# Two more feed-forward groups as seven block products, with low-part buffers of their own, another home for one sum, and reordered closings

## The chip, the cores and the metric

One core of a Trainium2 chip runs the whole program. The metric is device time in microseconds for one execution, lower is better. The kernel before was timed three times: 2315.58, 2322.17 and 2316.37 us, median 2316.37 us.

## The reference

The computation is a two-layer decoder trunk on 512 tokens of width 1024, all in float32. Every layer applies half a SwiGLU feed-forward, a token mixer, cross-attention into 256 memory tokens, and another half SwiGLU. The change is in the first half of the feed-forwards:

```python
def swiglu(x, w_gate, w_up, w_down):
    return (jax.nn.silu(x @ w_gate) * (x @ w_up)) @ w_down

def half_ffn(h, l, j):
    y = swiglu(rms_norm(h, ffn_norm_pre[l, j]), ffn_w_gate[l, j], ffn_w_up[l, j], ffn_w_down[l, j])
    return h + 0.5 * rms_norm(y, ffn_norm_post[l, j])
```

There are four feed-forwards, (layer, half) = (0,0), (0,1), (1,0), (1,1), with 2816 hidden columns each. Cross-attention uses `rms_norm(mem, mem_g) @ w_kv` in both layers, so the memory tokens are needed once in each layer.

## The kernel before

**Precision.** Each float32 operand is split into a high and a low part, and each product is three matmuls: low x high, high x low, high x high (lines 2447 to 2449 and 2565 to 2570). A weight tile of 128 x 1024 numbers (a "piece") is loaded into one of four raw slots, ScalarE copies its high part into `whi`, and the low part goes into `wlo`; both have four slots. Usually VectorE makes the low part as raw minus high (line 1503). ScalarE and VectorE split a piece three pieces ahead of TensorE (LOOKAHEAD).

**Groups.** The hidden columns are taken 256 at a time, so a feed-forward has eleven groups, in three stages: groups 0 to 2, groups 3 to 5, groups 6 to 10. After each of the first two stages a "quads" pass multiplies its three groups into the output (also by seven block products). Pass 0 is the opening pass, where ScalarE copies five of its products out of PSUM (line 1283) and VectorE adds the others (line 1599). After the third stage comes the plain down projection.

A plain group is 4 pieces of 24 matmuls of 512 columns, 96 in all. A group as seven block products ("woven") is 7 units of 24 matmuls of 256 columns, 168 in all. Before, groups 6 to 10 of the feed-forwards (0,1), (1,0) and (1,1) are woven, 15 groups in all.

**A woven group.** TensorE's units are, in order, B11, T1, T2, B21, T3, B22, T4. Four raw loads feed them, B11, B12, B22, B21, each of two DMAs of 256 KB on SyncE's queue. T1 to T4 are sums that VectorE makes in place in the raw slots (lines 1522, 1526, 1530, 1535: T1 = B12 - B11, T2 = B22 - T1, T3 = T2 - B11, T4 = B21 - T2). Before, T1, T2 and T4 all live in B12's slot. The next load into a slot waits for the last thing made from it.

The low parts of T1 to T4 are made by VectorE. Those of B11, B21 and B22 are made by DMA: ScalarE writes the negated and rounded copy of raw into the `wlo` slot (line 896) and the high part into `whi` (line 899); then GpSimd issues a DMA that adds raw onto the negated copy (line 792, "an add"), which leaves the low part. Each add moves 512 KB.

Between units, ScalarE copies three products out of PSUM ("keep", line 1195, after B11, T1 and T2). TensorE waits for the first before T2, for the third before T3, and for VectorE's sum c22 (line 2023) before T4. At a group's end ScalarE applies silu to the last product (line 1220) and VectorE multiplies (line 2036, "the product"). ScalarE's first keep of the next group waits for that product. In stage three ScalarE then splits the product at once (`plain_hi`, line 1163); in stage two VectorE would first make four block sums (lines 1944 to 1950), and ScalarE and VectorE split two parts (lines 1168, 1173, 1955, 1961).

**Order around the change.** Every engine runs its own list in program order, and SyncE's DMAs are issued in program order too. While the loads of the second group of stage two are issued, SyncE also issues the nine "corner" loads of the coming quads pass (w11, w12, w21, three DMAs of 256 KB each, line 624): w11's behind the group's first load, w12's behind the second, w21's behind the third.

**Closings.** Before the feed-forwards (0,1), (1,0) and (1,1) a closing finishes the sublayer row tile by row tile: VectorE updates h (line 1719), multiplies by the gain (1727) and forms the input variance (1760), GpSimd raises it to -1/2 (line 797; line 787 for the result's own variance), ScalarE scales the rows (988), TensorE transposes them (2529).

Of the kernel before, what the change touches and what calls it, by code (L numbers as in the profile page):

```python
# [35 lines left out]
D = 1024  # L36
SEQ = 512
MEM = 256
# [21 lines left out]
N_FF = FF // 256  # L60
MID_SLOTS = QUADS
S1, S2, S3, S4, A12, A22, A11 = range(7)
WOVEN = (6, 7, 8, 9, 10)
WOVEN_UNITS = ("B11", "T1", "T2", "B21", "T3", "B22", "T4")
WOVEN_SUMS = ("T1", "T2", "T3", "T4")
WOVEN_CORNERS = ("B11", "B12", "B22", "B21")
# [63 lines left out]
O_BANK = [6, 7, 4, 5]  # L130


def build(nc, A, out, h_kept):
    f32, f32r, bf16, i8 = mybir.dt.float32, mybir.dt.float32r, mybir.dt.bfloat16, mybir.dt.int8
    ALU, ACT, AX = mybir.AluOpType, mybir.ActivationFunctionType, mybir.AxisListType
    MUL, ADD, SUB = ALU.mult, ALU.add, ALU.subtract
# [31 lines left out]
    wlo = place("wlo", [P, SPLIT_SLOTS, PK, GC], f32r)  # L168
    memT_at = top[0]
    memT = place("memT", [P, KT, MEM])  # L170
    ring_at = top[0]
    ring = place("ring", [P, 4, SEQ])
    y_scratch = place("y_scratch", [P, 2, GC], f32, ring_at)
# [116 lines left out]
    raw_full = [sem(f"raw_full{i}") for i in range(RAW_SLOTS)]  # L290

    hi_made, lo_made, pieces_used = map(sem, ("hi_made", "lo_made", "pieces_used"))
    raw_added = [sem(f"raw_added{i}") for i in range(SPLIT_SLOTS)]
    corners_summed, s_made, s_hi_ready, s_lo_ready = map(sem, ("corners_summed", "s_made", "s_hi_ready", "s_lo_ready"))
    h_stored, h_back = sem("h_stored"), sem("h_back")
    product_kept, c11_ready, c11_silu, c22_ready = map(sem, ("product_kept", "c11_ready", "c11_silu", "c22_ready"))
# [51 lines left out]
    S_HELD_IN = [R22, R11, R21, R12]  # L348
    S_MADE = [0, 2, 1, 3]
    S_HIGH_AT = [6, 7, 8, 9]  # L350
    s_low = lambda s: s_lo_early[:, s] if s < 3 else s_lo_last[:]


# [75 lines left out]
        return slice(g * GC, (g + 1) * GC)  # L429

    raw_of, raw_split, passes = [], [], []
    sum_at, corner_unit, corner_raw, lo_by_dma, woven_base, woven_group = {}, {}, {}, set(), [], {}
    for n_stage, (kind, l, arg, ng, n) in enumerate(STAGES):
        if kind != "quads":
            for g in range(ng):
                if not woven(kind, l, arg, g):
                    for _ in range(group_pieces(kind, g, n, arg, l)):
                        raw_of.append(len(raw_split))
                        raw_split.append((len(raw_of) - 1,))
                    continue  # L440
                base, raw0 = len(raw_of), len(raw_split)
                unit = {name: base + i for i, name in enumerate(WOVEN_UNITS)}
                corner = {name: raw0 + i for i, name in enumerate(WOVEN_CORNERS)}
                held_in = {"B11": "B11", "B21": "B21", "B22": "B22", "T1": "B12", "T2": "B12", "T3": "B11", "T4": "B12"}
                raw_of += [corner[held_in[name]] for name in WOVEN_UNITS]
                raw_split += [(unit["T3"],), (unit["T4"],), (unit["B22"],), (unit["B21"], unit["T4"])]
                for name in WOVEN_SUMS:
                    sum_at[unit[name]] = len(sum_at) + 1, name, unit, corner
                lo_by_dma |= {unit[name] for name in WOVEN_BY_DMA}
                woven_group[n_stage, g] = len(woven_base)  # L450
                woven_base.append(base)
            continue
        place_of = lambda name, q: len(raw_of) + piece_of(quad_units().index((name, q)))
        passes.append((len(raw_of), len(raw_split), FF_GROUPS[arg[1]][0]))
        raw_split += [(place_of("B22", min(q + 1, QUADS - 1)),) for q in range(0, QUADS, 2)]
        raw_of += [None] * n

    def woven_first_of(w):
# [3 lines left out]
    def await_lo(eng, n):  # L462

        if n in lo_by_dma:
            eng.wait_ge(raw_added[n % SPLIT_SLOTS], 16 * sum(m in lo_by_dma for m in range(n % SPLIT_SLOTS, n + 1, SPLIT_SLOTS)))
        else:
            eng.wait_ge(lo_made, RAW_SLOTS + sum(m not in lo_by_dma for m in range(n + 1)))

# [112 lines left out]
    def _(sp):  # L581
# [18 lines left out]
        def load(n, halves):  # L600


            slot = n % RAW_SLOTS
            if n >= RAW_SLOTS:
                for m in raw_split[n - RAW_SLOTS]:
                    await_lo(sp, m)
            for dst, src in halves(slot):
                sp.dma_start(dst, src).then_inc(raw_full[slot], 16)

# [61 lines left out]
        def keep_h():  # L671

            kept[0] += 1
            sp.wait_ge(rows_scaled, TT * kept[0])
            for half in range(2):
                sp.dma_start(h_kept[half * HALF:(half + 1) * HALF].rearrange("(t p) d -> p t d", p=P),
                             h[:, 2 * half:2 * half + 2, :]).then_inc(h_stored, 16)

        def restore_h():

            sp.wait_ge(h_stored, 32 * kept[0])
            for half in range(2):
                sp.dma_start(h[:, 2 * half:2 * half + 2, :],
                             h_kept[half * HALF:(half + 1) * HALF].rearrange("(t p) d -> p t d", p=P)).then_inc(h_back, 16)

        kept = [0]
        piece = ended = loads = 0
# [82 lines left out]
    def _(pool):  # L770
# [17 lines left out]

        def add_raw(n):

            pool.wait_ge(hi_made, n + 1)
            g.dma_start(wlo[:, n % SPLIT_SLOTS], raw[:, raw_of[n] % RAW_SLOTS], accum_op=ADD).then_inc(raw_added[n % SPLIT_SLOTS], 16)

        def input_power(t):

# [38 lines left out]
        for n_stage, (kind, l, arg, ng, np_) in enumerate(STAGES):  # L834
            base_piece = E.piece
            for n in range(base_piece, base_piece + stage_pieces(kind, l, arg, ng, np_)):
                if n in lo_by_dma:
                    add_raw(n)
            E.piece += stage_pieces(kind, l, arg, ng, np_)
            if from_h(kind, arg) and not scaled_rows(kind, l, arg):  # L840
                power(TT, 0, rstd_in, var_in)
            if base_piece == 0:
                power(MT, 8)
            if kind == "even_in":
                make_tables()


                power(16)
                for _ in range(4):
                    power(TT)  # L850
                E.made[ring_summed.name] += KT
                E.seen[ring_squared.name] += KT
            elif kind == "odd_in":
                E.await_(conv_ready)
                for c in range(1, CONV_T):
                    E.await_(conv_ready)
                    if c > 1:
                        E.own()
                    E.run(g.tensor_tensor(ring[:, 0, :], conv[:, 0, :] if c == 1 else ring[:, 0, :], conv[:, c, :],
                                          ADD), conv_added)  # L860
                power(TT)
                E.made[ring_summed.name] += CONV_T
                E.seen[ring_squared.name] += CONV_T
            elif ends_sublayer(kind, arg) and opens_scaled(n_stage):
                power(1, 0)
                input_power(0)
                power(1, 1)
                input_power(1)
                power(1, 2)
                power(1, 3)  # L870
                input_power(2)
                input_power(3)
            elif ends_sublayer(kind, arg):
                for t in range(TT):
                    power(1, t)
# [3 lines left out]
    def _(act):  # L879
# [3 lines left out]
        def split(n):  # L883
# [8 lines left out]
            else:  # L892
                await_raw(act, raw_of[n])
            act.wait_ge(pieces_used, n + 1)
            if n in lo_by_dma:
                a(flat(wlo[:, slot]), flat(raw[:, from_slot]), ACT.Copy, scale=-1.0)  # L896
            gains = piece_gain[n]
            if gains is None:
                a(flat(whi[:, slot]), flat(raw[:, from_slot]), ACT.Copy).then_inc(hi_made, 1)  # L899
# [2 lines left out]
            for k, c in enumerate(gains):  # L902
                last = a(hi[:, k, :], full[:, k, :], ACT.Copy, scale=vec[:, c:c + 1])  # L903
            last.then_inc(hi_made, 1)

        def split_units(n, slot):

# [148 lines left out]
                softplus_last[0] = E.last  # L1056

        def memory_input(l, ks=range(KT)):
            for k in ks:
                E.run(a(m_hi[l % 2][:, k, :], memT[:, k, :], ACT.Copy,  # L1060
                        scale=vec[:, MEM_G + l * KT + k:MEM_G + l * KT + k + 1]), m_hi_ready)
# [421 lines left out]
    def _(dve):  # L1483
# [29 lines left out]
        def sum_corners(n):  # L1513
# [15 lines left out]
                dve.wait_ge(corners_summed, count - 1)  # L1529
                ins = v.tensor_tensor(flat(b11), flat(b12), flat(b11), SUB)  # L1530
            if name == "T4":
                await_raw(dve, corner["B21"])
                await_lo(dve, unit["T2"])
                dve.wait_ge(corners_summed, count - 1)
                ins = v.tensor_tensor(flat(b12), flat(b21), flat(b12), SUB)
            ins.then_inc(corners_summed, 1)

        def split_next():
# [125 lines left out]
        def close_sublayer(kind, n, n_stage):  # L1664
# [96 lines left out]
            if opens_scaled(n_stage):  # L1761
# [2 lines left out]
                row_variance(0)  # L1764
                update(1, take(1))
                gain_rows(1)
                split_next()
                row_variance(1)
                open_lo(0, x_banks[0])
                split_next()  # L1770
                open_lo(1, x_banks[1])
# [1 line left out]
                add_second(3)  # L1773
                update(2, made)
                gain_rows(2)
                made = weigh(3)
                row_variance(2)
                E.await_(input_rstd_ready, TT - 1)
                update(3, made)
                gain_rows(3)  # L1780
                split_next()
                row_variance(3)
                E.seen[input_rstd_ready.name] += 1
                split(E.piece + LOOKAHEAD)
# [656 lines left out]
    def _(pe):  # L2441
# [334 lines left out]
        def weave(w, bank):  # L2776
# [8 lines left out]
            def unit(name, bank, start, stop):  # L2785
                n = base + WOVEN_UNITS.index(name)
                weights(n)
                wh, wl = [t[:, n % SPLIT_SLOTS].rearrange("p a (b n) -> p (a b) n", n=256) for t in (whi, wlo)]
                if name in corner_of:
                    hi, lo = [token_half(t, *corner_of[name]) for t in (xhi, xlo)]  # L2790
                else:
# [395 lines left out]
```

## Time and profile before

| | us |
|---|---|
| median of 3 runs | 2316.37 |
| the profiled execution, own time | 2316.41 |
| its span (first to last instruction) | 2314.6 |
| TensorE busy in it | 2270.2 (98%) |
| VectorE busy | 1464.9 (63%) |
| ScalarE busy | 1061.6 (46%) |
| GpSimd busy | 115.0 (5%) |

How to read it: times are microseconds from the first instruction. PE is TensorE, DVE VectorE, ACT ScalarE, POOL GpSimd, SP SyncE. A matmul's duration includes its pipeline, so the distance from one start to the next, and not the duration, tells what it costs; an idle time in brackets runs from the modelled end of the instruction before.

### The profile page before, as it was taken

How to read it: one execution, taken by the hardware profiler on the slowest of the kernel's cores; microseconds unless marked ns; L12 is line 12 of the kernel's file. 1: busy time of each engine (PE TensorE's matmuls, PEld its weight loads, DVE VectorE, ACT ScalarE, POOL GpSimd, SP SyncE). 2: the span in 40 equal slices, each digit the busy share in tenths (PEclk: the TensorE clock that was granted, in tenths of full speed). 3: DMA queues.
4: the chain of work that ended last, by engine and by line, in shares of the span. 5: the costliest groups of instructions: out<-in, count | busy, mean ns of one | idle time of the engine just before them, and what ended most of it. 6: DMA issues, size and time to landing. Idle time of an engine off the chain costs nothing. (4 is left out here: it accounts for less than half of the span.)

```text
span 2314.6 us, 32573 instructions
## 1 busy us (share of the span) xinstructions
PE 2270.2 (98%) x12963; PEld 1972.9 (85%) x12963; DVE 1464.9 (63%) x1898; ACT 1061.6 (46%) x1642; POOL 115.0 (5%) x160
## 2 busy tenths in 40 slices
PE   8999999999999999999999999999999999999998
PEld 7888888888888888889878889988878888888997
DVE  5857445595655558476557566555997575766664
ACT  5433334444544444345544436535265554443652
POOL 0000004000000000001010001100000000000100
PEclk9999999999999999999999999999999999999999
DMA  4332332311223232417634316642322212431672
GB/s 168 119 119 82 100 101 83 106 59 56 83 74 105 78 120 90 149 49 179 170 118 164 123 54 146 169 155 90 112 72 84 92 64 94 152 123 60 155 191 110
DMA packets 181837, 255.61 MB, mean 110 GB/s; under 512 B 14040, under 2 KB 123960, under 8 KB 181688
## 3 DMA queue, kind: packets, MB, share of 16 engines
q1 hardware_dynamic: 175096, 229.90, 30.6%
q0 software_dynamic: 6480, 23.60, 5.3%
q8 instruction: 104, 1.70, 0.3%
q14 instruction: 45, 0.37, 0.0%
q10 hardware_dynamic: 112, 0.03, 0.0%
HBM read 221.50 MB, written 8.39 MB: 99 GB/s over the span
## 5 line engine op out<-in xcount | busy, mean ns | idle before, releaser
L2447 PE MATMUL ps<-xlo,whi 128*128 128x512 f32 (+1 forms) x1936 | 672.0, 347 | 22.2 <-DMA wlo<-raw 15.5
L2448 PE MATMUL ps<-xhi,wlo 128*128 128x512 f32 (+1 forms) x1936 | 668.3, 345 | 0.0
L2449 PE MATMUL ps<-xhi,whi 128*128 128x512 f32 (+1 forms) x1936 | 668.0, 345 | 0.0
L1503 DVE TENSOR_TENSOR wlo<-raw,whi 128x1024 fp32r<-128x1024 f32 x236 | 287.8, 1223 | 319.2 <-ACT whi L899 317.3
L899 ACT ACTIVATE whi<-raw 128x1024 fp32r<-128x1024 f32 x281 | 295.3, 1054 | 398.3 <-PE ps L2449 295.7
L2447 PEld LDWEIGHTS ps<-xlo,whi 128*128 128x128 f32 x1936 | 367.2, 190 | 70.5 <-issue 20.8
L2449 PEld LDWEIGHTS ps<-xhi,whi 128*128 128x128 f32 x1936 | 367.2, 190 | 44.1
L2448 PEld LDWEIGHTS ps<-xhi,wlo 128*128 128x128 f32 x1936 | 367.4, 190 | 43.7
L1509 DVE SCALAR_TENSOR_TENSOR wlo<-raw,vec,whi 128x512 fp32r<-128x512 f32 (+1 forms) x224 | 154.9, 737 | 154.2 <-ACT whi L903 153.5
L903 ACT ACTIVATE whi<-raw,vec 128x512 fp32r<-128x512 f32 (+1 forms) x224 | 145.4, 702 | 198.0 <-PE ps L2449 163.2
L2447 PE MATMUL ps<-wlo,xhi 128*128 128x512 f32 x352 | 138.6, 394 | 1.0 <-issue 1.0
L2449 PE MATMUL ps<-whi,xhi 128*128 128x512 f32 x352 | 137.1, 390 | 0.0
L2448 PE MATMUL ps<-whi,xlo 128*128 128x512 f32 x352 | 137.0, 389 | 0.0
L2448 PE MATMUL ps<-s_hi,wlo 128*128 128x256 f32 x480 | 135.8, 283 | 0.0
L2449 PE MATMUL ps<-s_hi,whi 128*128 128x256 f32 x480 | 135.8, 283 | 0.0
L2565 PE MATMUL ps<-wlo,mid_hi 128*128 128x512 f32 x336 | 131.7, 392 | 0.4 <-DVE wlo L1494 0.4
L2570 PE MATMUL ps<-whi,mid_hi 128*128 128x512 f32 x336 | 130.8, 389 | 0.0
L2569 PE MATMUL ps<-whi,mid_lo 128*128 128x512 f32 x336 | 130.8, 389 | 0.0
L2447 PE MATMUL ps<-wlo,plain_hi 128*128 128x512 f32 x320 | 125.1, 391 | 0.0
L2449 PE MATMUL ps<-whi,plain_hi 128*128 128x512 f32 x320 | 124.6, 389 | 0.0
L2448 PE MATMUL ps<-whi,plain_lo 128*128 128x512 f32 x320 | 124.5, 389 | 0.0
L922 ACT ACTIVATE whi<-w 128x512 fp32r<-128x512 f32 x144 | 83.2, 622 | 88.3 <-PE ps L2449 29.6
(321 smaller groups left out, 3750.7 us busy)
## 6 DMA issues: line engine op xcount, KB each, us to landing
raw<-ffn_w_gate_dram SPq DMA_DIRECT2D x176, 256.0 KB, 3.0
raw<-ffn_w_up_dram SPq DMA_DIRECT2D x176, 256.0 KB, 3.1
raw<-ffn_w_down_dram SPq DMA_DIRECT2D x96, 256.0 KB, 3.2
wlo<-raw POOLq DMA_DIRECT2D x45, 512.0 KB, 4.8
w<-ffn_w_down_dram SPq DMA_DIRECT2D x72, 256.0 KB, 5.3
raw<-xattn_w_kv_dram SPq DMA_DIRECT2D x64, 256.0 KB, 3.0
raw<-even_w_in_dram SPq DMA_DIRECT2D x56, 256.0 KB, 2.9
raw<-odd_w_in_dram SPq DMA_DIRECT2D x42, 256.0 KB, 2.9
```

The lines of the kernel that those rows point to most:

```text
L899: a(flat(whi[:, slot]), flat(raw[:, from_slot]), ACT.Copy).then_inc(hi_made, 1)
L903: last = a(hi[:, k, :], full[:, k, :], ACT.Copy, scale=vec[:, c:c + 1])
L922: last = a(whi[:, slot, i, :], unit_source(k, name, q), ACT.Copy)
L1503: v.tensor_tensor(flat(wlo[:, slot]), flat(raw[:, from_slot]), flat(whi[:, slot]).bitcast(f32), SUB).then_inc(lo_made, 1)
L1509: last = v.scalar_tensor_tensor(out=lo[:, k, :], in0=full[:, k, :], scalar=vec[:, c:c + 1], in1=hi[:, k, :].bitcast(f32), op0=MUL, op1=SUB)
L2447: mm(out_ap, lh, rl, start=start, stop=False, skip_group_check=skip_group_check)
L2448: mm(out_ap, ll, rh, start=False, stop=False, skip_group_check=skip_group_check)
L2449: return mm(out_ap, lh, rh, start=False, stop=stop, skip_group_check=skip_group_check)
L2565: opening = mm(out, hi, wlo[:, slot, i, :], start=fresh, stop=False, skip_group_check=True)
L2569: mm(out, lo, whi[:, slot, i, :], start=False, stop=False, skip_group_check=True)
L2570: last = mm(out, hi, whi[:, slot, i, :], start=False, stop=ends, skip_group_check=True)
```

## The change

Six edits come together. (1) Groups 3 and 4 of the three feed-forwards are woven too. (2) Two new low buffers, `lo_aside`, take the low parts of B11 and B21 in place of the `wlo` slots; they lie where `memT` (the transposed memory tokens, 1 MB) was, so memT is stored to DRAM in the first stage of (0,1) and loaded back at the end of (1,0). (3) The add waits for the negated copy alone, not for the high part too; B21's negated copy is made one unit earlier, in front of T2's high part. (4) T4 is made in B21's slot, so B12's slot is free for the next load as soon as T4's sum is made, and the sum T4 waits for B21's add. (5) Adds have a semaphore for each of the three names. (6) In the closings before a scaled feed-forward, VectorE forms the input variance of rows 1 and 2 earlier, and one split moves ahead of the update of row 3; GpSimd's power of row 2's input comes ahead of that of row 3's result.

```diff
-WOVEN = (6, 7, 8, 9, 10)
+WOVEN = (3, 4, 6, 7, 8, 9, 10)
...
     memT = place("memT", [P, KT, MEM])
+    lo_aside = place("lo_aside", [P, 2, PK, GC], f32r, memT_at)
...
+    low_part = lambda n: lo_aside[:, lo_by_dma[n][1]] if n in lo_by_dma and lo_by_dma[n][1] < 2 else wlo[:, n % SPLIT_SLOTS]
...
-                held_in = {..., "T3": "B11", "T4": "B12"}
+                held_in = {..., "T3": "B11", "T4": "B21"}
-                raw_split += [(unit["T3"],), (unit["T4"],), (unit["B22"],), (unit["B21"], unit["T4"])]
+                raw_split += [("lo", unit["T3"]), ("sum", unit["T4"]), ("lo", unit["B22"]), ("lo", unit["T4"])]
...
+            if kept[0] == 1:
+                sp.wait_ge(m_lo_ready, KT)
+                sp.dma_start(mem_kept.rearrange("(k p) n -> p k n", p=P), memT[:]).then_inc(mem_stored, 16)
...
+            if l == 1 and arg[0] == 0:
+                sp.wait_ge(mem_stored, 16)
+                sp.dma_start(memT[:], mem_kept.rearrange("(k p) n -> p k n", p=P)).then_inc(mem_back, 16)
...
         def add_raw(n):
-            pool.wait_ge(hi_made, n + 1)
-            g.dma_start(wlo[:, n % SPLIT_SLOTS], raw[:, raw_of[n] % RAW_SLOTS], accum_op=ADD)...
+            w, i = lo_by_dma[n]
+            pool.wait_ge(negated, len(WOVEN_BY_DMA) * w + i + 1)
+            g.dma_start(low_part(n), raw[:, raw_of[n] % RAW_SLOTS], accum_op=ADD).then_inc(raw_added[i], 16)
...
                 power(1, 2)
+                input_power(2)
                 power(1, 3)
-                input_power(2)
                 input_power(3)
...
             act.wait_ge(pieces_used, n + 1)
-            if n in lo_by_dma:
-                a(flat(wlo[:, slot]), flat(raw[:, from_slot]), ACT.Copy, scale=-1.0)
+            for m in (n, n + 1):
+                if m in lo_by_dma and (m == n) == (lo_by_dma[m][1] != 1):
+                    negate(m)
...
+        def negate(n):
+            w, i = lo_by_dma[n]
+            await_raw(act, raw_of[n])
+            if i < 2 and w:
+                act.wait_ge(pieces_used, woven_base[w - 1] + WOVEN_UNITS.index(WOVEN_BY_DMA[i]) + 1 + SPLIT_SLOTS)
+            if (w, i) == (0, 0):
+                act.wait_ge(mem_stored, 16)
+            a(flat(low_part(n)), flat(raw[:, raw_of[n] % RAW_SLOTS]), ACT.Copy, scale=-1.0).then_inc(negated, 1)
...
             if name == "T4":
-                await_raw(dve, corner["B21"])
+                await_lo(dve, unit["B21"])
                 await_lo(dve, unit["T2"])
-                ins = v.tensor_tensor(flat(b12), flat(b21), flat(b12), SUB)
+                ins = v.tensor_tensor(flat(b21), flat(b21), flat(b12), SUB)
...
                 gain_rows(1)
+                row_variance(1)
                 split_next()
-                row_variance(1)
...
                 gain_rows(2)
+                row_variance(2)
                 made = weigh(3)
-                row_variance(2)
+                split_next()
                 E.await_(input_rstd_ready, TT - 1)
                 update(3, made)
                 gain_rows(3)
-                split_next()
                 row_variance(3)
```

## Rows read from the trace of the kernel before

**Rows 1.** The page, part 1: busy time, share and instructions of each engine.
```profile
PE 2270.2 (98%) x12963; PEld 1972.9 (85%) x12963; DVE 1464.9 (63%) x1898; ACT 1061.6 (46%) x1642; POOL 115.0 (5%) x160
```

**Rows 2.** Waits of TensorE: line, awaited engine and line, us, times, longest.
```profile
PE ps L2447 <- DMA wlo<-raw: 15.7, 12, 3.1
...
PE ps L2447 <- DVE c L2023: 2.6, 2, 1.3
PE ps L2529 <- ACT y_rows L988: 2.2, 3, 1.8
PE ps L2447 <- DVE wlo L1503: 2.1, 3, 1.5
```

**Rows 3.** Timeline of TensorE (start, duration): first group 3 matmul of (0,1), next pass.
```profile
940.99 0.39 PE L2447 MATMUL ps<-xlo,whi 128*128 128x512 f32 x1
...
1006.27 0.39 PE L2565 MATMUL ps<-wlo,mid_hi 128*128 128x512 f32 x1
```

**Rows 4.** Timeline of TensorE, stage three of each feed-forward: first B11, last T4.
```profile
1034.93 0.28 PE L2447 MATMUL ps<-xlo,whi 128*128 128x256 f32 x1
...
1054.96 0.28 PE L2449 MATMUL ps<-xhi,whi 128*128 128x256 f32 x1
...
1142.55 0.28 PE L2447 MATMUL ps<-xlo,whi 128*128 128x256 f32 x1
...
1397.26 0.29 PE L2447 MATMUL ps<-xlo,whi 128*128 128x256 f32 x1
...
1505.27 0.28 PE L2447 MATMUL ps<-xlo,whi 128*128 128x256 f32 x1
...
2146.61 0.28 PE L2447 MATMUL ps<-xlo,whi 128*128 128x256 f32 x1
...
2249.86 0.28 PE L2447 MATMUL ps<-xlo,whi 128*128 128x256 f32 x1
```

**Rows 5.** The page, part 3: DMA queues, packets, MB, share of 16 engines' span.
```profile
q1 hardware_dynamic: 175096, 229.90, 30.6%
q0 software_dynamic: 6480, 23.60, 5.3%
```

**Rows 6.** Windows: length, busy time of five engines, granted clock, DMA share, GB/s.
```profile
940.00:952.00 12.00, 12.00 (x55) 9.93 (x54) 3.68 (x3) 3.56 (x4) 0.00 (x0) 1.00 1.01 344
...
1464.20:1468.00 3.80, 3.80 (x20) 3.80 (x21) 2.25 (x3) 2.95 (x3) 0.85 (x1) 0.57 0.00 0
```

**Rows 7.** Timeline of VectorE in the first woven group of (0,1).
```profile
1037.54 0.69 DVE L1599 TENSOR_TENSOR y_rows<-ps,y_rows 128x512 f32<-128x512 f32 x1
...
1040.79 1.22 DVE L1503 TENSOR_TENSOR wlo<-raw,whi 128x1024 fp32r<-128x1024 f32 x1 [1.13 <-ACT whi L899]
```

**Rows 8.** DMAs issued at 1063.05, 1065.60, 1070.94, 1071.52: KB, us to landing.
```profile
raw<-ffn_w_gate_dram SPq DMA_DIRECT2D x1, 256.0 KB, 2.8
...
wlo<-raw POOLq DMA_DIRECT2D x1, 512.0 KB, 4.4
...
wlo<-raw POOLq DMA_DIRECT2D x1, 512.0 KB, 8.5
...
raw<-ffn_w_gate_dram SPq DMA_DIRECT2D x1, 256.0 KB, 8.4
```

**Rows 9.** Timeline of ScalarE in the second woven group of (0,1), start 1056.79.
```profile
1057.36 1.05 ACT L896 ACTIVATE wlo<-raw 128x1024 fp32r<-128x1024 f32 x1
...
1060.20 0.59 ACT L1195 ACTIVATE c<-ps 128x512 f32<-128x512 f32 x1
...
1068.64 1.06 ACT L896 ACTIVATE wlo<-raw 128x1024 fp32r<-128x1024 f32 x1 [1.33 <-PE ps L2449]
...
1079.93 1.06 ACT L896 ACTIVATE wlo<-raw 128x1024 fp32r<-128x1024 f32 x1 [1.34 <-DMA raw<-ffn_w_gate_dram]
```

**Rows 10.** Timeline of GpSimd in the first closing before a scaled feed-forward.
```profile
836.58 0.54 POOL L797 TENSOR_TENSOR rstd_in<-var_in,neg_half 128x1 f32<-128x1 f32 x1 [3.94 <-DVE var_in L1760]
...
850.56 1.45 POOL L797 TENSOR_TENSOR rstd_in<-var_in,neg_half 128x1 f32<-128x1 f32 x1 [3.86 <-DVE var_in L1760]
```

More of the change, by code:

```diff
@@ L130, with build @@
 O_BANK = [6, 7, 4, 5]
-def build(nc, A, out, h_kept):
+def build(nc, A, out, h_kept, mem_kept):
     f32, f32r, bf16, i8 = mybir.dt.float32, mybir.dt.float32r, mybir.dt.bfloat16, mybir.dt.int8
@@ L292, in build @@
     hi_made, lo_made, pieces_used = map(sem, ("hi_made", "lo_made", "pieces_used"))
-    raw_added = [sem(f"raw_added{i}") for i in range(SPLIT_SLOTS)]
+    raw_added = [sem(f"{name.lower()}_added") for name in WOVEN_BY_DMA]
+    negated, mem_stored, mem_back = map(sem, ("negated", "mem_stored", "mem_back"))
     corners_summed, s_made, s_hi_ready, s_lo_ready = map(sem, ("corners_summed", "s_made", "s_hi_ready", "s_lo_ready"))
@@ L431, in build @@
     raw_of, raw_split, passes = [], [], []
-    sum_at, corner_unit, corner_raw, lo_by_dma, woven_base, woven_group = {}, {}, {}, set(), [], {}
+    sum_at, lo_by_dma, woven_base, woven_group = {}, {}, [], {}
     for n_stage, (kind, l, arg, ng, n) in enumerate(STAGES):
@@ L438, in build @@
                         raw_of.append(len(raw_split))
-                        raw_split.append((len(raw_of) - 1,))
+                        raw_split.append(("lo", len(raw_of) - 1))
                     continue
@@ L443, in build @@
                 corner = {name: raw0 + i for i, name in enumerate(WOVEN_CORNERS)}
-                held_in = {"B11": "B11", "B21": "B21", "B22": "B22", "T1": "B12", "T2": "B12", "T3": "B11", "T4": "B12"}
+                held_in = {"B11": "B11", "B21": "B21", "B22": "B22", "T1": "B12", "T2": "B12", "T3": "B11", "T4": "B21"}
                 raw_of += [corner[held_in[name]] for name in WOVEN_UNITS]
-                raw_split += [(unit["T3"],), (unit["T4"],), (unit["B22"],), (unit["B21"], unit["T4"])]
                 for name in WOVEN_SUMS:
                     sum_at[unit[name]] = len(sum_at) + 1, name, unit, corner
-                lo_by_dma |= {unit[name] for name in WOVEN_BY_DMA}
+                raw_split += [("lo", unit["T3"]), ("sum", unit["T4"]), ("lo", unit["B22"]), ("lo", unit["T4"])]
+                for i, name in enumerate(WOVEN_BY_DMA):
+                    lo_by_dma[unit[name]] = len(woven_base), i
                 woven_group[n_stage, g] = len(woven_base)
@@ L454, in build @@
         passes.append((len(raw_of), len(raw_split), FF_GROUPS[arg[1]][0]))
-        raw_split += [(place_of("B22", min(q + 1, QUADS - 1)),) for q in range(0, QUADS, 2)]
+        raw_split += [("lo", place_of("B22", min(q + 1, QUADS - 1))) for q in range(0, QUADS, 2)]
         raw_of += [None] * n
@@ L464, in await_lo @@
         if n in lo_by_dma:
-            eng.wait_ge(raw_added[n % SPLIT_SLOTS], 16 * sum(m in lo_by_dma for m in range(n % SPLIT_SLOTS, n + 1, SPLIT_SLOTS)))
+            w, i = lo_by_dma[n]
+            eng.wait_ge(raw_added[i], 16 * (w + 1))
+            eng.wait_ge(hi_made, n + 1)
         else:
@@ L604, in load @@
             if n >= RAW_SLOTS:
-                for m in raw_split[n - RAW_SLOTS]:
+                made, m = raw_split[n - RAW_SLOTS]
+                if made == "lo":
                     await_lo(sp, m)
+                else:
+                    sp.wait_ge(corners_summed, sum_at[m][0])
             for dst, src in halves(slot):
@@ L789, in add_raw @@
         def add_raw(n):
-            pool.wait_ge(hi_made, n + 1)
-            g.dma_start(wlo[:, n % SPLIT_SLOTS], raw[:, raw_of[n] % RAW_SLOTS], accum_op=ADD).then_inc(raw_added[n % SPLIT_SLOTS], 16)
+            w, i = lo_by_dma[n]
+            pool.wait_ge(negated, len(WOVEN_BY_DMA) * w + i + 1)
+            g.dma_start(low_part(n), raw[:, raw_of[n] % RAW_SLOTS], accum_op=ADD).then_inc(raw_added[i], 16)
         def input_power(t):
@@ L904, in split @@
             last.then_inc(hi_made, 1)
+        def negate(n):
+            w, i = lo_by_dma[n]
+            await_raw(act, raw_of[n])
[4 more added lines that the diff above has]
+            a(flat(low_part(n)), flat(raw[:, raw_of[n] % RAW_SLOTS]), ACT.Copy, scale=-1.0).then_inc(negated, 1)
         def split_units(n, slot):
@@ L1058, in memory_input @@
         def memory_input(l, ks=range(KT)):
+            if l == 1 and 0 in ks:
+                act.wait_ge(mem_back, 16)
             for k in ks:
@@ L2787, in unit @@
                 weights(n)
-                wh, wl = [t[:, n % SPLIT_SLOTS].rearrange("p a (b n) -> p (a b) n", n=256) for t in (whi, wlo)]
+                wh, wl = [t.rearrange("p a (b n) -> p (a b) n", n=256) for t in (whi[:, n % SPLIT_SLOTS], low_part(n))]
                 if name in corner_of:
@@ L3183 @@
     h_kept = nc.dram_tensor("h_kept", (SEQ, D), mybir.dt.float32).ap()
-    build(nc, tensors, out, h_kept)
+    mem_kept = nc.dram_tensor("mem_kept", (D, MEM), mybir.dt.float32).ap()
+    build(nc, tensors, out, h_kept, mem_kept)
     r = run_bass_kernel_spmd(nc, [arrays], core_ids=[0])
```

## The prediction

> **What bounds the kernel now.** The page's first part comes first: TensorE is busy for 2270.2 of 2314.6 us [rows 1], so what TensorE computes and the few places where it waits set the time. The view of its waits then names these: 15.7 us for adds onto the low slots, 2.6 us for VectorE's c22, and 2.2 + 2.1 us in the closings [rows 2]. Its timeline gives the prices. The three plain groups of stage two run from 940.99 to 1006.27 [rows 3], 21.76 us each, 0.2267 us for each of 96 matmuls. In a woven group 168 starts lie 0.12 apart (1034.93 to 1054.96 is 167 steps [rows 4]), so it costs 20.15 us undisturbed. Stage three lasts from its first B11 to its last T4 plus 24 x 0.12 = 2.88 us: 110.5, 110.9 and 106.1 us [rows 4], against 5 x 20.15 = 100.8. So 25 us are lost there, and the adds are 15.7 + 12 x 0.16 = 17.6 of them (an idle time starts at the modelled end, 0.28 after a start, where the next start would have come at 0.12).
>
> The sum is made against the profiled execution's own 2316.41 us, 1.8 more than its span; the median of the runs is 2316.37, so nothing has to be shifted. From no change this kernel can be told at about 0.3%, 7 us.
>
> **The change, part by part.**
>
> *Matmuls.* Six groups go from 21.76 to 20.15 us: -1.6 each, -9.7 us, all on TensorE's path.
>
> *The second woven group of stage two (group 4).* I count from the start of group 3's B11. What is late here is the load of B21 for group 4, and ScalarE stands behind it.
> SyncE may load into B11's slot when T3's low part exists. In a first woven group that is 1040.79 + 1.22 - 1034.93 = 7.1 us after the start [rows 7]; after the opening pass ScalarE, not VectorE, takes the last two products, two additions of 0.69 [rows 7] less, so about 5.9. From there SyncE's list is B11 (2 DMAs), w11 (3), B12 (2), w12 (3), then, once group 3's B22 add has landed, B22 (2), w21 (3), B21 (2): 17 DMAs of 256 KB. Together with that add and the next B11's they are all the DMA engines' work until B21 is there. A DMA of 256 KB costs all engines 0.76 us by the saturated stretch (344 GB/s at a share of 1.01 [rows 6]) and 0.81 by the queue's share (30.6% of 2314.6 us for 229.9 MB [rows 5]); I take 0.78, 13.3 us for 17. An add costs 5.3% x 2314.6 / 45 = 2.7 us [rows 5], 5.4 for two. First bytes come 2.8 - 0.8 = 2.0 us after an issue [rows 8]. So B21 lands at 5.9 + 2.0 + 13.3 + 5.4 = 26.6.
> ScalarE now writes B21's negated copy in front of T2's high part, and waits for the load there, as it already did once in its old place (1.34 us [rows 9]). Behind it stand, in order: negated copy 0.95, T2 high 0.95 (copies follow each other at 0.95 [rows 9]), T2 low 1.2, product 0.7 [rows 7], block high at most 0.95, first keep 0.6 [rows 9]: 5.35, and TensorE's T2 can start at 32.0. Undisturbed it starts at 20.15 + 2 x 2.88 = 25.9. TensorE is 6.1 late, and some 0.6 more where T3 waits for the third keep, which the block sums hold up. The pair of groups gains 3.2 and loses 6.7: +3.5 for each feed-forward, +10.5 for three, and without the matmuls' -9.7 that is +20.
> Bounds: if adds took no engine time, B21 lands at 21.2, T2 is 0.7 late and the pair gains 2.5, -7.5 in all. Where four loads and an add ran together, 3.1 + 2.7 = 5.8 us of work took from 1072 to 1079.9 [rows 8], 7.9; by that rate another 2 us are lost per pair, +17 in all. The saturated stretch is the nearest row, so +10.5.
> An idle time of 2.8 us before 1464.2 was followed by 3.8 us at a granted clock of 0.57 [rows 6], the 1.2 GHz level, where 20 matmuls took 1.6 us more. Waits of 4 to 6 us stand in three pairs; I add +2 (0 to +5).
>
> *Stage three.* Taken away: the add of the next B11 starts 1.2 us earlier (the negated copy ends at 1069.7, the issue was at 1070.94, after the high part [rows 8, 9]); twelve waits for adds come to 15.7 us, the longest 3.1 [rows 2]; with up to 1.2 off each I leave 6 of them, so 9.7 go, and 8 x 0.16 with those that vanish. The two c22 waits (2.6 + 0.3) go, since B12 loads sooner, and the clock's 1.6: in all about -15. Put in: B12's load now comes before or with the add of B22 and no longer after it. That add was alone (4.4 [rows 8]) and landed 13.2 us into the group; TensorE wants it at 14.4. Issued 1.1 earlier, at 7.7, and slowed by two to four loads it takes between 4.4 and 8.5 [rows 8]. I take 7.5 for the twelve groups that load a successor: 15.2, 0.8 late each, +10. Then T2 stands behind B21's load as above: landing at 23.1 before (1071.52 + 8.4 - 1056.79 [rows 8]), about 1.1 sooner now, plus 5.4, against 25.9 + 0.8: 0 to 0.8 each, +3. Sum -2; bounds -15 (the add stays at 4.4) and +8 (8.5 each).
>
> *Closings.* The wait of 2.1 for a low part [rows 2] goes, because that split now runs before row 3's update; row 3's update starts 0.8 later, but has slack. Row 1's variance moves ahead of a split. GpSimd's power takes 0.54 alone and 1.45 when a split starts beside it [rows 10], so moving it 1.1 earlier gives only 0.2 of the 2.2 [rows 2]. -2 (-5 to +2).
> The Trainium skill, SBUF — State Buffer, section Who interferes with whom, says that a VectorE instruction with two SBUF inputs and a GpSimd instruction that reads SBUF block each other; by the 0.54 row alone this closing term would be -5, by the rule and the 1.45 row it is the -2.
>
> *Memory tokens.* The store and the load back, 1 MB each, are 3 us of DMA work, hidden under plain groups whose loads run pieces ahead: 0 (uncovered, at most +3 each).
>
> Sum: 2316.4 - 9.7 + 20.2 + 2 - 2 - 2 = 2325 us.
>
> **Rivals.** *Forecast:* B21's late load holds ScalarE in group 4; 2325, own range 2318 to 2336; chance 0.45.
> *Faster, the other side:* group 4's loads overlap better. It decides at a landing of 25.9 - 5.3 = 20.6 us: sooner, and T2 isn't late. For it: adds need no HBM, and the waits on adds are the largest in the trace. Against it: 17 loads alone end at 21.2. Price: pairs -9.7 + 2, stage three -12, closings -2: 2294; chance 0.20.
> *Stage three gives all it can:* the pairs lose as forecast, but B22's add stays near 4.4, and stage three returns 13: 2316.4 + 10.5 - 13 - 2 = 2312; chance 0.27. For it: every add starts 1.1 us or more earlier; against it: 8.5 us beside four loads [rows 8].
> The Trainium skill, DMA: Bandwidth & Descriptors, section Queues, rings and completion order, has each engine take turns between its queues packet by packet. An add of 144 packets would then pass at most 144 packets of loads, 0.6 us, and end at 5.0; that is this rival, and the 8.5 speaks against it.
> *The wait only moves, and grows:* B22 takes 1.5 us in all twelve groups (+6), pairs +14, the clock falls in each (+3), closings -1: 2338; chance 0.08.
>
> **How the numbers follow.** The likeliest is 2325. The range 2300 to 2337 leaves out the lower half of the faster case and the upper half of the last: 0.16. Within 0.3% (2309.4 to 2323.3) lie most of the third case and the lower edge of the forecast, 0.31; faster 0.24; slower 0.45.
>
> **What would show it.** Right: in the trace after, TensorE waits 3 to 6 us before T2 of group 4 in three places, ScalarE before it on a load of `ffn_w_gate`; the list of waits has the adds at under 15 us although there are 63 instead of 45, and B22's (with `s_lo_last`) among them; 256-column matmuls rise by 6 x 168. Wrong: groups 3 and 4 last under 42 us together, or stage three under 103 us.

## The result: 1.2% slower, 2344.0 us

The changed kernel takes 2344.01 us, the median of 4 runs (2341.56 to 2349.97), against 2315.97 for the kernel before in the same rounds (4 runs, 2313.81 to 2322.17): a ratio of 1.0116, 95% interval 1.0096 to 1.0136. The prediction had 2325 and a range that ended at 2337. Its side was right, the size was not.

The profiled execution is 2341.56 us, 25.15 more than the 2316.41 of before. Stage by stage, read as in [rows 3] and [rows 4] (from the first matmul of a stage to the first of the next; stage three from its first B11 to its last T4 plus 24 x 0.12):

| us | before | after | difference | predicted |
|---|---|---|---|---|
| groups 3 and 4, three pairs | 130.56 | 150.77 | +20.2 | +12.5 (-9.7 matmuls, +20.2 stalls, +2 clock) |
| stage three, three times | 327.52 | 334.36 | +6.8 | -2 |
| closings | | | -2.4 | -2 |
| first wait for input rows | 6.7 | 7.2 | +0.5 | 0 |

**The profile after.** The page's part 1, part 3 and, of part 6, the adds (operation, count, KB, median us to landing). They answer to [rows 1], [rows 5] and [rows 8]:

```profile
PE 2270.9 (97%) x13395; PEld 1992.0 (85%) x13395; DVE 1507.5 (64%) x1946; ACT 1103.8 (47%) x1702; POOL 131.6 (6%) x178
...
q1 hardware_dynamic: 177176, 232.00, 30.4%
q0 software_dynamic: 9072, 33.03, 7.7%
...
lo_aside<-raw POOLq DMA_DIRECT2D x42, 512.0 KB, 4.4
...
wlo<-raw POOLq DMA_DIRECT2D x21, 512.0 KB, 7.0
```

TensorE is as busy as before, so the 25 us are idle time. Those onto `lo_aside` are the adds of B11 and B21; those onto `wlo` are B22's, and they are slow: 7.0 us in the median. TensorE's waits, to be held against [rows 2]:

```profile
PE ps L2476 <- DMA wlo<-raw: 21.7, 20, 2.3
PE ps L2476 <- ACT c L1224: 17.2, 13, 4.2
...
PE ps L2476 <- DVE c L2052: 5.6, 3, 2.7
PE ps L2558 <- ACT y_rows L1015: 3.1, 5, 1.6
```

No wait is left for B11's or B21's add, but B22's add is waited for 20 times. The 13 waits for kept products (line 1224) stand against a single one before:

```profile
PE ps L2447 <- ACT c L1195: 0.4, 1, 0.4
```

TensorE's timeline through the pair of (0,1), start and duration in us, then the same pair's last matmul and the next group's first; in brackets the idle time before an instruction and what ended it:

```profile
940.93 0.28 PE L2476 MATMUL ps<-xlo,whi 128*128 128x256 f32 x1
...
957.28 0.38 PE L2476 MATMUL ps<-s_lo_last,whi 128*128 128x256 f32 x1 [1.79 <-DMA wlo<-raw]
...
963.07 0.39 PE L2476 MATMUL ps<-xlo,whi 128*128 128x256 f32 x1 [2.66 <-DVE c L2052]
...
974.10 0.39 PE L2476 MATMUL ps<-s_lo_early,whi 128*128 128x256 f32 x1 [0.64 <-ACT c L1224]
...
985.23 0.39 PE L2476 MATMUL ps<-s_lo_last,whi 128*128 128x256 f32 x1 [1.73 <-DMA wlo<-raw]
...
990.96 0.28 PE L2478 MATMUL ps<-xhi,whi 128*128 128x256 f32 x1
991.08 0.40 PE L2476 MATMUL ps<-xlo,whi 128*128 128x512 f32 x1
```

Those with a wait are, in order, group 3's B22, its T4, group 4's T2, its B22. T4 waits for VectorE, which has group 4's first sum ahead of c22 in its list and waits there for B12's tile:

```profile
961.19 1.23 DVE L1551 TENSOR_TENSOR raw<-raw 128x1024 f32<-128x1024 f32 x1 [7.78 <-DMA raw<-ffn_w_up_dram]
962.33 0.68 DVE L2052 TENSOR_TENSOR c<-ps,c 128x512 f32<-128x512 f32 x1
```

In the other two pairs, of (1,0) and (1,1), T2 of group 4 waits longest:

```profile
1343.58 0.58 PE L2476 MATMUL ps<-s_lo_early,whi 128*128 128x256 f32 x1 [4.23 <-ACT c L1224]
...
2098.78 0.58 PE L2476 MATMUL ps<-s_lo_early,whi 128*128 128x256 f32 x1 [4.11 <-ACT c L1224]
```

Before T2 stands ScalarE, as forecast. Its timeline in the pair of (0,1), and then in the second group of stage three, which began at 1062.90:

```profile
962.45 1.06 ACT L916 ACTIVATE whi<-raw 128x1024 fp32r<-128x1024 f32 x1 [7.23 <-DVE raw L1551]
968.81 1.06 ACT L931 ACTIVATE lo_aside<-raw 128x1024 fp32r<-128x1024 f32 x1 [5.30 <-DMA raw<-ffn_w_gate_dram]
969.78 1.04 ACT L916 ACTIVATE whi<-raw 128x1024 fp32r<-128x1024 f32 x1
...
1064.88 1.06 ACT L931 ACTIVATE lo_aside<-raw 128x1024 fp32r<-128x1024 f32 x1 [4.51 <-DMA raw<-ffn_w_gate_dram]
...
1069.81 0.58 ACT L1224 ACTIVATE c<-ps 128x512 f32<-128x512 f32 x1
...
1071.71 1.06 ACT L931 ACTIVATE wlo<-raw 128x1024 fp32r<-128x1024 f32 x1
```

Line 931 is the negated copy. B21's (968.81, 1064.88) waits 5.30 and 4.51 us for a load, and everything else of ScalarE waits with it, B22's negated copy (1071.71) included. What follows in that second group of stage three: GpSimd issues B22's add, which lands 7.8 us later, and TensorE waits before T2 and before B22 (1080.86).

```profile
1073.06 0.87 POOL L808 DMA_DIRECT2D wlo<-raw  x1 [5.97 <-ACT wlo L931]
wlo<-raw POOLq DMA_DIRECT2D x1, 512.0 KB, 7.8
```

```profile
1070.44 0.39 PE L2476 MATMUL ps<-s_lo_early,whi 128*128 128x256 f32 x1 [1.62 <-ACT c L1224]
...
1080.86 0.39 PE L2476 MATMUL ps<-s_lo_last,whi 128*128 128x256 f32 x1 [1.52 <-DMA wlo<-raw]
```

### The profile page after: what moved, and what is told of

The parts are those of the page before. It is cut to its first block and busy times, and to the rows that moved or that the text cites. A ratio compares the mean times of both kernels' runs of the same rounds, so it can differ in the third digit from the quotient of the medians.

```text
span 2339.8 us, 33744 instructions
## 1 busy us (share of the span) xinstructions
PE 2270.9 (97%) x13395; PEld 1992.0 (85%) x13395; DVE 1507.5 (64%) x1946; ACT 1103.8 (47%) x1702; POOL 131.6 (6%) x178
## 3 DMA queue, kind: packets, MB, share of 16 engines
q1 hardware_dynamic: 177176, 232.00, 30.4%
q0 software_dynamic: 9072, 33.03, 7.7%
## 5 line engine op out<-in xcount | busy, mean ns | idle before, releaser
L2476 PE MATMUL ps<-xlo,whi 128*128 128x512 f32 (+1 forms) x1888 | 638.0, 338 | 7.3 <-DVE c L2052 5.6
L2478 PE MATMUL ps<-xhi,whi 128*128 128x512 f32 (+1 forms) x1888 | 634.1, 336 | 0.0
L2477 PE MATMUL ps<-xhi,wlo 128*128 128x512 f32 (+1 forms) x1552 | 539.2, 347 | 0.0
L1532 DVE TENSOR_TENSOR wlo<-raw,whi 128x1024 fp32r<-128x1024 f32 x236 | 288.3, 1224 | 293.5 <-ACT whi L916 290.7
L916 ACT ACTIVATE whi<-raw 128x1024 fp32r<-128x1024 f32 x299 | 314.0, 1053 | 344.3 <-PE ps L2478 230.7
L2477 PEld LDWEIGHTS ps<-xhi,wlo 128*128 128x128 f32 x1552 | 294.6, 190 | 36.1
L2477 PE MATMUL ps<-s_hi,wlo 128*128 128x256 f32 x672 | 192.0, 286 | 0.0
L2478 PE MATMUL ps<-s_hi,whi 128*128 128x256 f32 x672 | 191.9, 286 | 0.0
L2476 PE MATMUL ps<-s_lo_early,whi 128*128 128x256 f32 x504 | 146.4, 290 | 17.5 <-ACT c L1224 17.2
L2477 PEld LDWEIGHTS ps<-s_hi,wlo 128*128 128x128 f32 x672 | 130.9, 195 | 0.0
L2478 PEld LDWEIGHTS ps<-s_hi,whi 128*128 128x128 f32 x672 | 130.8, 195 | 0.0
```

The costliest lines, as they stand in the source:

```text
L1532: v.tensor_tensor(flat(wlo[:, slot]), flat(raw[:, from_slot]), flat(whi[:, slot]).bitcast(f32), SUB).then_inc(lo_made, 1)
L2476: mm(out_ap, lh, rl, start=start, stop=False, skip_group_check=skip_group_check)
L2477: mm(out_ap, ll, rh, start=False, stop=False, skip_group_check=skip_group_check)
L2478: return mm(out_ap, lh, rh, start=False, stop=stop, skip_group_check=skip_group_check)
```

## The experiments

Theory: the loss has two parts that TensorE's order ties together. B21's negated copy, made one split early, holds ScalarE until B21's tile lands, so T2's first product is kept late. And B22's add starts late, is slow beside the next group's loads, and frees B22's tile late, which the next T2 needs too. Rivals: the pairs are simply short of DMA work, or T4's new home (which lets B12 load sooner) is to blame. A short name stands for each run; times are medians, the ratio is to the kernel before in the same rounds, the last two columns are sums over three feed-forwards in the profiled execution.

| run | us | ratio (95%) | pairs | stage three |
|---|---|---|---|---|
| before | 2316 | 1 | 130.6 | 327.5 |
| changed kernel | 2344.0 | 1.0116 | 150.8 | 334.4 |
| e1 groups 3, 4 plain | 2323.8 | 1.0023 (1.0011 to 1.0036) | 130.6 | 337.1 |
| e2 B21's copy in place | 2326.9 | 1.0040 (1.0025 to 1.0055) | 139.1 | 331.7 |
| e3 T4 in B12 | 2342.1 | 1.0101 (1.0082 to 1.0120) | 148.2 | 338.4 |
| e4 corners later | 2341.4 | 1.0100 (1.0082 to 1.0118) | 139.2 | 342.0 |
| e5 before, 3 and 4 woven | 2328.4 | 1.0043 (1.0025 to 1.0061) | 142.6 | 320.1 |
| e6 e2 and e3 | 2316.1 | 1.0002 (0.9989 to 1.0015) | 138.1 | 322.0 |
| e7 own buffer for B22 | 2300.0 | 0.9925 (0.9906 to 0.9944) | 138.0 | 304.7 |
| e8 B22 by VectorE | 2296.4 | 0.9911 (0.9895 to 0.9926) | 130.0 | 309.1 |
| f1 e7 and e4 | 2283.7 | 0.9849 (0.9831 to 0.9866) | 121.4 | 305.7 |
| f2 e7, 3 and 4 plain | 2293.8 | 0.9889 (0.9871 to 0.9906) | 130.6 | 305.7 |
| f3 e7, and e8 in 3 and 4 | 2293.8 | 0.9891 (0.9874 to 0.9908) | 131.3 | 306.1 |
| f4 f3 and e4 | 2285.2 | 0.9853 (0.9831 to 0.9874) | 123.0 | 304.2 |

Undisturbed, the pairs would be 3 x 2 x 20.15 = 120.9 and stage three 3 x 5 x 20.15 = 302.3. The profiled execution of e5 took 2323.7 us, the shortest of its five, so its columns lie under what its median would give.

**e1, groups 3 and 4 left plain.**

```diff
-WOVEN = (3, 4, 6, 7, 8, 9, 10)
+WOVEN = (6, 7, 8, 9, 10)
```

> The changed kernel with groups 3 and 4 left as plain groups; every other edit stays. Theory (the pairs of groups 3 and 4 carry most of the loss, +20 of 25 us, and stage three the rest, +7): the pairs are back at 43.5 us each, stage three stays at 110 to 113 us per feed-forward, closings 2.4 us shorter than before; 2319 to 2323 us, 0.1 to 0.3% slower than before. Rival (the edits of stage three are worth something, and stage three is only longer because the pairs end late or leave loads behind): stage three at 103 to 108 us per feed-forward, 2300 to 2312 us.

Measured 2323.8, just above the theory's range. Stage three (113.8, 109.5 and 113.8 us) is 9.6 us longer than before although the groups ahead of it are plain, as before. So the edits harm stage three by themselves, and the pairs are the larger part of the loss.

**e2, B21's negated copy at its own split.**

```diff
-            for m in (n, n + 1):
-                if m in lo_by_dma and (m == n) == (lo_by_dma[m][1] != 1):
-                    negate(m)
+            if n in lo_by_dma:
+                negate(n)
```

> The changed kernel with B21's negated copy made again at B21's own split, not one split early. Theory A (ScalarE stands behind B21's late raw tile before T2's product is kept): TensorE's waits for kept products (17.2 us in 13 waits) fall to under 5 us; if nothing takes their place 2330 us, and 2335 if half of it turns into waits for B21's add, which now starts later. Theory B (T2 is late because B21 is late for everything behind it): those waits turn into waits for B21's add or for T4's sum one for one, 2340 to 2345 us.

The pairs fall by 11.7 us, stage three by 2.6, and the time by 17. That is below the expected 2330, so theory A holds for the pairs, though the waits for kept products fell to 9.9 us and not under 5. The waits that remain are of both kinds:

```profile
PE ps L2475 <- DMA wlo<-raw: 11.2, 13, 1.5
PE ps L2475 <- ACT c L1223: 9.9, 8, 1.9
```

T2 is still late, though its product no longer stands behind B21. In group 4 of (0,1) ScalarE now waits 4.64 us for VectorE's sum T2, which needs B22's tile, and that tile loads only when the last group's B22 add has landed:

```profile
966.76 1.06 ACT L915 ACTIVATE whi<-raw 128x1024 fp32r<-128x1024 f32 x1 [4.64 <-DVE raw L1554]
```

**e3, T4 in B12's tile again.**

```diff
-  "T4": "B21"}
+  "T4": "B12"}
-  raw_split += [("lo", unit["T3"]), ("sum", unit["T4"]), ("lo", unit["B22"]), ("lo", unit["T4"])]
+  raw_split += [("lo", unit["T3"]), ("lo", unit["T4"]), ("lo", unit["B22"]), ("lo", unit["B21"])]
```

(and T4's sum written to B12's tile as before).

> The changed kernel with T4 made in B12's raw tile again, so that the next group's B12 loads after T4 is split and not after T4 is summed. Theory A (B22's add is slow because the next B12's load now runs beside it): the add of B22 (onto wlo) falls from 7.0 us to 4.4 to 5.5, the 21.7 us of waits for it fall to under 8, stage three is 104 to 108 us per feed-forward; 2318 to 2330 us. Theory B (the add is slow because the next B11 and w11 load beside it, which needs no new home of T4): the add stays at 6.5 us or more, the time within 5 us of the changed kernel's 2342.

Half of theory A came true and none of its time: B22's add fell to 5.9 us (between the two theories) and the waits for it from 21.7 to 2.0, but T2's rose to 24.1 and those for c22 to 11.1:

```profile
PE ps L2476 <- ACT c L1224: 24.1, 11, 4.9
PE ps L2476 <- DVE c L2052: 11.1, 12, 2.2
...
PE ps L2476 <- DMA wlo<-raw: 2.0, 4, 0.9
```

**e6, both.**

> Both at once: B21's negated copy at its own split and T4 in B12's tile. Theory A (two chains are late side by side in stage three, B22's slow add and T2's product behind B21's copy, and mending one shows the other): the sum of stage three, 331.7 and 338.4 us with one mended, is 322 to 328 with both, pairs 45 to 47 each; 2318 to 2325 us. Theory B (the two edits are independent): T4's home brings nothing again, 2325 to 2331 us.

Theory A, and a little better than its range. In stage three, where e2 brought 2.6 us and e3 cost 4.0, both together bring 12.4: each of the two chains had hidden what mending the other was worth.

**e4, corner loads with group 5.**

```diff
-  if piece and after in pass_of and g == (2 if n == 0 else 1) and kp < 3:
+  if piece and after in pass_of and g == 2 and kp < 3:
```

> The changed kernel with the corner loads for the quadrant products that follow stage two issued with group 5, not with groups 1 and 2 ahead of groups 3 and 4. Theory A (every DMA ahead of or beside group 4's raw tiles counts, so the pair is short of DMA work): the pairs fall from 50.1 us to 41 to 46 each, 2318 to 2332 us. Theory B (group 4 waits on a chain of group 3, T3's low part, the add of B22 and the tile that it frees, not on the queue's length): the pairs stay within 1.5 us of 50, 2338 to 2346 us.

Neither in full. The pairs fall by 11.6 us (46.7, 44.9 and 47.6, two of them above theory A's 46), so the DMA work around them counts; the time does not fall by as much, since stage three grows by 7.6. Whether that was waits for B22 is what f1 asks.

**e5, the kernel before with groups 3 and 4 woven.**

> The kernel before with groups 3 and 4 woven as well, and none of the other edits. Theory A (the pair is short of DMA work wherever its low parts lie): pairs of 49 to 51 us as in the changed kernel, stage three as before (327 us in three), 2334 to 2340 us. Theory B (B21's negated copy ahead of its split is most of the pair's loss): pairs of 45 to 47 us, 2321 to 2328 us.

The time is just above theory B's range, and so are two of the three pairs. The pairs cost 47.5 us each on average, against 50.3 in the changed kernel and 46.4 in e2. In every arrangement that leaves B22's low part and the corner loads where they were, a woven pair is dearer than a plain one (43.5). Stage three is 7.4 us shorter than before in this run; that is not explained.

**e7, the own low buffers to B11 and B22.**

```diff
-  lo_aside[:, lo_by_dma[n][1]] if n in lo_by_dma and lo_by_dma[n][1] < 2
+  lo_aside[:, lo_by_dma[n][1] // 2] if n in lo_by_dma and lo_by_dma[n][1] != 1
-  (m == n) == (lo_by_dma[m][1] != 1)
+  (m == n) == (lo_by_dma[m][1] != 2)
-  if i < 2 and w:
+  if i != 1 and w:
```

> The changed kernel with the own low buffers given to B11 and B22 in place of B11 and B21: B21's negated copy is made in its slot at its own split, B22's one split early, in front of T3's high part, so that its add starts 2 to 3 us earlier. Theory A (B22's add, 6 to 8.5 us long, is late at its use, and it also frees B22's tile late for the next group's T2): no waits for B22 are left, T2's waits fall under 5 us in all, pairs 42 to 45 us, stage three 103 to 108 us; 2297 to 2313 us. Theory B (the DMA engines are short of time, so an add that starts earlier ends as late or delays the loads beside it): waits for adds stay at 10 us or more, now on B21 or B11 too, 2320 to 2332 us.

Theory A. Stage three loses 29.7 us and is within 2.4 of undisturbed; only 2 waits are left in it. The pairs, at 138.0, are hardly under e2's 139.1, two of the three above the forecast: their largest waits are before B11 of group 4 (2.18 and 2.70 us, to which the profile names no releaser; they end where B11's add lands), and that add takes 8.3 to 9.4 us beside the corner loads.

**e8, B22's low part by VectorE.**

```diff
-WOVEN_BY_DMA = ("B11", "B21", "B22")
+WOVEN_BY_DMA = ("B11", "B21")
```

(with e2's edit).

> The changed kernel with B21's negated copy at its own split, and B22's low part made by VectorE (1.22 us) as for the sums, without a copy and an add: 42 adds in place of 63. Theory A (VectorE has room, 70 of 112 us busy in stage three, and the add is the trouble): the 11 us of waits for B22 go, T2's waits halve; 2306 to 2318 us. Theory B (VectorE stands in order behind it with T4's sum and the block sums): waits for c22 and for T4 grow by 8 us or more, 2324 to 2336 us.

Better than theory A: VectorE had the room, c22's waits fell to 1.3 us, and with 42 adds for 63 the pairs are 9.1 us shorter than in e2, as cheap as plain ones, and stage three 22.6.

**f1 to f4, put together.** f1 is e7's and e4's edits. f2 is e7 with e1's. f3 leaves B22 out of `lo_by_dma` in groups 3 and 4 of e7. f4 is f3 with e4's.

> Own low buffers for B11 and B22, and the corner loads issued with group 5. Theory A (the loss that the later corner loads put into stage three, 341.96 against 334.36 us, was waits for B22, and those are mended): pairs of 40.5 to 43 us each, stage three 101 to 103 us each, 2288 to 2295 us. Theory B (the corner loads delay whatever runs beside them, now the first groups of stage three): pairs as good, but stage three at 104 us or more, 2296 to 2304 us.

> Own low buffers for B11 and B22, groups 3 and 4 plain. Theory A (with the buffers in these places the pairs still cost 138.0 against 130.6 us, so that all of the gain is stage three's): 2290 to 2295 us, 5 to 10 us less than with the pairs woven. Theory B (a plain group 5 ahead of stage three after plain groups 3 and 4 leaves stage three's first loads later): stage three above 104 us, 2297 us or more.

> Own low buffers for B11 and B22 in stage three, and in groups 3 and 4 B22's low part made by VectorE. Theory A (each stage takes the way that was better for it): pairs of 43 to 43.7 us, stage three 101 to 102 us, 2289 to 2295 us. Theory B (the stages are not independent, since the better one hands its lateness on): 2297 to 2302 us.

> The same with the corner loads issued with group 5. Theory A (what is left of the pairs' loss, 2.7 to 3.4 us each, is group 4's B11 add and its T2 behind corner loads): pairs of 40.4 to 42 us, stage three 101 to 103 us, 2282 to 2290 us. Theory B (corner loads only change the place where they are in the way): 2291 to 2298 us.

Theory A in f2 and f4; f1 came out 4 us better than its range, and in f3 the time fits, but a pair (44.7) and stage three are a little over. Stage three in f1 is 1.0 us longer than in e7, where the same edit cost 7.6 in e4: that loss hung on B22's late add. f1 against f2 is what weaving groups 3 and 4 is worth once nothing is late: 9.2 us of pairs, of 9.7 possible. f1 and f4 can't be told apart, so with later corner loads VectorE's way has nothing to add. f1 beats both kernels: 1.5% under before. Its pair of (0,1) in TensorE's timeline lasts 40.56 us, and its list of waits has no add and no kept product left:

```profile
941.33 0.28 PE L2476 MATMUL ps<-xlo,whi 128*128 128x256 f32 x1
...
981.89 0.40 PE L2476 MATMUL ps<-xlo,whi 128*128 128x512 f32 x1
```

```profile
PE ps L2476 <- issue: 3.4, 5, 1.2
PE ps L2558 <- ACT y_rows L1015: 3.1, 5, 1.6
```

The reason, on ScalarE in its second group of stage three (start 1053.42): B21's negated copy waits for nothing, and B22's comes at 3.7 us into the group, where the changed kernel has it at 8.8.

```profile
1053.20 1.05 ACT L931 ACTIVATE wlo<-raw 128x1024 fp32r<-128x1024 f32 x1
...
1057.13 1.05 ACT L931 ACTIVATE lo_aside<-raw 128x1024 fp32r<-128x1024 f32 x1
```

The add issued behind it, at 1058.47, lands 4.9 us later, 9.9 us into the group; TensorE wants it at 14.4.

## Why the prediction was right on the side and wrong on the size

*Matmuls, -9.7.* Right: an undisturbed pair in f1 takes 40.32 us, from 1291.16 to 1331.48, twice 20.15.

*Group 4, +20.2 of stalls and +2 of clock.* The mechanism is the one forecast, step by step: B21's copy waits for a gate load and starts 27.9 us after group 3's B11 (968.81 - 940.93; 26.6 predicted), T2 starts at 33.2 (32.0 predicted), e2 takes 11.7 us of it away. Most of the 1.3 us between 26.6 and 27.9 is the start of the loads, 7.0 us after B11 and not 5.9; the text's own sum, 7.1 less twice 0.69, is 5.7. Of the three waits of 3 to 6 us before T2 two came; in (0,1) the waits for B22 and c22 had taken most of the lateness before. Stalls and clock came to 29.9 us. The clock is 6.3 of them, three times the 2 that was taken and above its bound of 5:

```profile
963.07:967.00 3.93, 3.93 (x20) 3.93 (x21) 2.84 (x3) 0.44 (x1) 0.00 (x0) 0.57 1.05 387
1343.58:1349.25 5.67, 5.67 (x26) 5.67 (x27) 5.42 (x6) 4.33 (x6) 0.40 (x1) 0.50 0.13 34
2098.78:2103.60 4.82, 4.82 (x22) 4.82 (x23) 4.56 (x6) 3.47 (x5) 0.00 (x0) 0.51 0.03 6
```

These windows (length, busy times, granted clock, DMA share, GB/s, as in [rows 6]) hold 20, 26 and 22 matmuls, which take 1.5, 2.6 and 2.2 us more than at 0.12 each. Without the clock the pairs are 13.9 over before, inside the bounds that the prediction gave (-7.5 and +17) and 3.4 above the +10.5 that it took. The upper bound itself was worked out wrongly: 7.9 us for 5.8 us of work, carried over "by that rate" to the 18.7 us ahead of B21, would be 6.8 us more per pair and not 2. What the prediction left out is what comes behind T2: B22's copy stands behind the late keeps on the same engine, and its add, 6.0 us beside the next loads, is late by another 1.73.

*Stage three, -2: the step that failed.* It was "Issued 1.1 earlier, at 7.7, and slowed by two to four loads it takes between 4.4 and 8.5 [rows 8]. I take 7.5". The duration was about right (6.7 to 8.2 us, 7.0 in the median). The issue was not: 8.5 us into the first group of (0,1) (1050.07 - 1041.54) and 10.2 into the second (1073.06 - 1062.90), where T2 itself waited 1.62, so there the add landed at 17.9 and not at 15.2. The prediction had seen that ScalarE stands behind B21's load, but charged that to T2 alone. It did not carry the delay on to B22's copy, which is queued on ScalarE behind T2's and T3's parts. B21's copy is only part of that delay. In e2, where it is back in its place, the add is issued at 7.8 to 8.0 in the first group of each feed-forward's stage three, near the forecast, but at 7.9 to 10.5 in the other twelve. In six of these T2's sum waits 1.7 to 3.2 us for B22's tile, which loads only behind the last group's B22 add. Stage three is only 2.6 us shorter. This loop ends where that add starts early (e7) or is gone (e8). So in the changed kernel B22 waits for 16.2 us in 15 waits and T2 for 8.3 in 10; counted as the prediction counts, with 0.16 more each, that is 28.5 us where 10 + 3 had been taken. The last group of each stage three, left out by the prediction since it loads no successor, holds 5.0 of B22's 16.2 in the three together. What was taken away came to about 21.7 (28.5 - 6.8) and not to 15, which hid a part of the error. The adds together made 21.7 us of waits where the text had put the limit at 15. In e1, without any pairs, stage three came out 9.6 over before, beyond the bound of +8.

*The rivals.* "The wait only moves, and grows", with a chance of 0.08, is what stage three did: B22 waits in all of its 15 groups, for 1.1 us on average. The 1.5 that it priced was too much, but its place was right and its sum came nearest: stage three +6 (measured +6.8), pairs +14 (+13.9 without the clock), and only the clock, +3, was well short (6.3). "Stage three gives all it can" fell with the add. The Trainium skill, DMA: Bandwidth & Descriptors, section Queues, rings and completion order, was cited for it, with an estimate of 5.0 us for an add. The changed kernel differs: B22's adds took 7.0 us in the median and none under 5.6. In e7 and f1, where they start earlier, they took 4.8 in stage three's median. "Faster" decided at a landing of 20.6 us; the copy that waits for it started at 27.9, and the kernels that did become faster did so by other edits. (The prediction's 0.16 for what its range leaves out should be 0.14, half of 0.20 and half of 0.08.)

*Closings, -2.* Measured -2.4: the 2.1 us for a low part [rows 2] is gone from the list, as forecast. That the total fits so well is partly luck: the waits for `y_rows` grew from 2.2 to 3.1, and one of 0.8 for VectorE's update of h went, of which the prediction had neither. *Memory tokens, 0.* The stretch from the end of stage three of (1,0) to the next mixer stage, in which the load back lies, is 341.1 us in both traces (1508.15 to 1849.25 before, 1521.96 to 1863.06 after).

## What to carry to other kernels

An operation put one step ahead in an in-order queue moves its wait for data ahead too, and everything behind it pays, also work that the move wasn't about: follow the delay to the last consumer in that queue, not only to the first. An own buffer belongs to the operand whose low part starts too late for its use: given to B22 in place of B21, with B22's copy made one unit earlier, the same 1 MB was worth another 27 us (e7 against e2, which both have B21's copy in its place). And where two chains end at the same consumer close together, undo both before judging either.

## What the runs showed of the hardware that was not expected

A packet of the adds' queue (q0) keeps a DMA engine about five times as long as one of the loads: 7.7% x 2339.8 us x 16 / 9072 packets = 0.32 us against 30.4% x 2339.8 x 16 / 177176 = 0.064. It also carries 2.8 times as many bytes (33.03 MB / 9072 against 232.00 MB / 177176), so byte for byte the add is 1.8 times as dear. Alone an add of 512 KB takes 4.4 us, beside the corner loads up to 9.8. Loads of 256 KB take 2.7 us when nothing is ahead of them (at 947.89) and up to 9.5 beside adds, but beside other transfers they reach 9.8 without an add too (at 1173.31). How much of it is the add's, and in what order an engine takes their packets, was not settled.

The granted clock did not follow the length of one wait. It was 0.50 (the 1.2 GHz level) after waits of 4.23 and 4.11 us and 0.57 after 2.66, but in e7 it stayed at 1.00 from 1318.00 to 1321.00 after a wait of 2.18, and in e2 it was 0.65 from 1335.54 to 1340.30 after a wait of 1.85, which followed two more of 1.53 and 1.01 from 1319 on. (0.57 and 0.65 are means of stretches that hold both levels.) In the kernel before it even stayed at 1.00 behind the longest wait of stage three, 3.09 us:

```profile
1125.21 0.36 PE L2447 MATMUL ps<-xlo,whi 128*128 128x256 f32 x1 [3.09 <-DMA wlo<-raw]
```

```profile
1125.21:1128.21 3.00, 3.00 (x25) 3.00 (x26) 2.33 (x2) 1.43 (x2) 0.86 (x1) 1.00 0.31 64
```
